# A hybrid decoder layer on one core: sample states as the fixed operand, and other orders in the MLP passages and the closing tiles

## The chip, the core and the metric

One core of a Trainium2 chip (trn2). The metric is the device time of one launch, in microseconds. A core has five engines with queues of their own that run strictly in order and wait for one another by semaphores: TensorE (PE in the profile; its weight loads are PEld), VectorE (DVE), ScalarE (ACT), GpSimd (POOL) and SyncE (SP), which only issues DMAs here.

## What is computed

A prompt of 1024 positions behind 16 learned meta positions, and 8 sample sequences that decode one position each, go through one layer: 1048 columns in all. All is float32.

```python
hn = rmsnorm(h, norm_mix);  z = hn @ w_in                 # D = 1024
u_in, c_gate, b_gate, q, k, v, g = split(z)
y_conv = b_gate * causal_conv3(c_gate * u_in)              # 512 channels
o, S = retention(rotary(q), rotary(k), v)                  # 4 heads of 128
   # prompt: chunks of 128; sample: S_b = gamma*S_b + k_b^T v_b; o_b = q_b S_b
y_ret = o * rsqrt(mean(o*o) + eps) * silu(g)               # norm per head
h = h + concat(y_conv, y_ret) @ w_out
h = h + square(relu(rmsnorm(h, norm_mlp) @ w_up)) @ w_down # D_FF = 4096
y = rmsnorm(h, norm_final)                                 # outputs, with states
```

## The kernel before

TensorE multiplies float32 in three products of a reduced format: each operand is split into a high part (ScalarE: a rounding copy) and a low part (VectorE or GpSimd: value minus high part), and hi*hi, lo*hi and hi*lo are added in PSUM.

**Heads.** A loop over four heads; each head has six units of projection times three column tiles, steps j = 0 to 17. In between stand the chunks of the retention. For the samples: ScalarE scales the eight states (j = 5), spreads the eight query columns over a table `q_smp` of 8 by 8 columns, zero off the diagonal (j = 6), and VectorE updates the states. At j = 12 TensorE runs eight float32 products with `q_smp[:, b, :]` (8 columns) as the fixed operand and a state (128 columns) as the moving one (L1748); they add up to an 8 x 128 tile, a sample a row. ScalarE copies it (L916), takes the sum of squares of each row (L917) and the roots (L922), VectorE scales it with the other rows (L1254, L1257), and TensorE turns it at j = 14 (L1760) together with nine prompt tiles (L1757). VectorE multiplies the turned tiles with the gate (L1265), for which ScalarE makes silu at j = 12, 13, 14 (L929).

**MLP.** Both projections are done as Strassen-like block products: seven products instead of eight per 2 x 2 block, here called steps i = 0 to 6. The up projection has 16 units q (`UNITS`); the down projection 8 blocks b of hidden channels (`BLOCKS`), each with four passages n (output channels), the list `DN`. So a down step has the number 7q + i, with q the passage. An up step is 24 products of 258 columns, a down step 12. A step writes into PSUM pair `BANK[i]`, (0, 1, 0, 1, 2, 1, 2), so step 2 waits until the result of step 0 has been read, step 3 for step 1, 5 for 3, 6 for 4, the next passage's 1 for 5.

The last block is cut by columns: passage n = 0 whole, then n = 1, 2, 3 for columns 0 to 258 of each half (`ts = (0,)`), then for 258 to 516.

Around each step the other engines work in an order that is written out by hand:
- ScalarE splits weights (`up_split`, `down_split`) and the middle values (`mid_split`), squares (`squared`), and reads step 0 of an up unit (L1079). `SPLITS` and `LOWS` say at which up step the weights of units 1 and 2 are split; later units follow one unit ahead. `mid_step` says at which down step the seven middle operands of the next block get their high part; the two halves of the low part (`mid_low`, VectorE, L1440) come one and two steps later. Down weights lie in two slots; those of passages 5 to 9 are split at the steps of `AHEAD`, 5.6 steps a passage, later ones two passages ahead.
- VectorE reads every step out of PSUM. In block 0 it copies step 0 into `a1` (L1581) and adds `h_in` to steps 1, 2, 3, 5 (L1585); in all other cases it adds to what is there (L1591). It also makes `mid_sum` (block sums of the middle values), `scaled` (relu and norm) and the low parts.
- GpSimd makes the block sums of the weights (L709 to L717 up, L743 to L748 down), the low parts of the down weights (L755), at the end `close` (L769: three of four results still need `a1`), and `gather` (L775).
- SyncE loads weights and middle values (`load_down`, `load_mid`) and stores.

**Closing tiles.** The result lies channel by channel; nine tiles `FINAL` of up to 128 positions are turned by eight transpositions each (L1870), squared and summed by ScalarE (L1128), rooted (L1133), and scaled by VectorE with the gain into `y_out` (L1557). Four tiles (columns 0 to 256 of both halves) run between the last products (`FINAL_AT`, `NORM_AT`), five after them, one of which gathers columns 496 to 516 of both halves.

```python
 87 FINAL_AT = {(NW, 3): 0, (NW + 1, 0): 1, (NW + 1, 5): 2, (NW + 2, 3): 3}
 88 NORM_AT = {(NW + 1, 1): 0, (NW + 1, 3): 1, (NW + 2, 1): 2, (NW + 2, 6): 3}
109     return {0: {4: 0}, 1: {1: 1, 4: 2}, 2: {1: 3, 4: 4}, 3: {1: 5, 4: 6}}[n]
136   AHEAD.setdefault(min(28 + (28 * (_wi - 5) + 4 * _i) // 5 + 1, 55), []).append((_wi, _i))
```

## Time and profile before

| | |
|---|---|
| three runs | 1168.94, 1171.07, 1172.07 us; median 1171.07 |
| profiled execution | 1170.56 us, its span 1168.8 us |
| TensorE busy | 1145.3 us, 98% of the span, 8689 products |
| weight loads (PEld) | 1119.8 us, 96% |
| VectorE, ScalarE, GpSimd busy | 764.9, 434.7, 551.0 us |
| mean granted clock | 0.996 |

The span is from the first to the last instruction. TensorE's products overlap: a product's record is 0.28 us long and the next starts 0.12 us after it, so "busy" only says that some record covers the time. A row of the timeline has start, length, engine, line, operation and tiles; in brackets, how long the engine was idle before it and who released it. Roughly: 0 to 60 us the input, to 390 the heads, to 482 the output projection, to 813 the up half, to 1154 the down half, then the closing tiles.

### The profile page before, as it was taken

The numbers are of one execution on the slowest core, as the hardware profiler recorded it, in microseconds if no ns is written. First come the engines' busy times: TensorE is split into PE (matmuls) and PEld (weight loads), VectorE is DVE, ScalarE is ACT, GpSimd is POOL, SyncE is SP. The second block draws the span as 40 slices with busy tenths as digits, with TensorE's granted clock in tenths as the row PEclk, the third lists the DMA queues.
The fourth block names the chain that finished last, engine by engine and source line by source line (L and its number), as shares of the span: only waits on it lengthen the run. The fifth ranks groups of instructions, "written<-read, shape, count | busy, mean of one in ns | idle before, by whom it ended". The sixth has DMA issues, their size and how long they took to land.

```text
span 1168.8 us, 22531 instructions
## 1 busy us (share of the span) xinstructions
PE 1145.3 (98%) x8689; PEld 1119.8 (96%) x8689; DVE 764.9 (65%) x1141; ACT 434.7 (37%) x853; POOL 551.0 (47%) x541
## 2 busy tenths in 40 slices
PE   9999999999999999989999999999999999999996
PEld 7899999999999999989999999999898999999996
DVE  4355446456355676787777776777866677777756
ACT  6423313214124433533333333335434444444413
POOL 0154242253150431044232322323989998888992
PEclk9999999999999999999999999999999999999999
DMA  6431211211201222254435353437854553454213
GB/s 202 132 110 36 79 50 54 74 54 54 74 19 57 80 89 87 74 163 134 166 118 181 109 166 130 138 120 257 277 186 129 177 169 103 146 176 136 89 38 146
DMA packets 154007, 139.79 MB, mean 120 GB/s; under 512 B 6809, under 2 KB 118146, under 8 KB 153916
## 3 DMA queue, kind: packets, MB, share of 16 engines
q1 hardware_dynamic: 148814, 135.50, 36.3%
q10 hardware_dynamic: 5102, 3.05, 0.9%
q8 instruction: 61, 1.00, 0.4%
q14 instruction: 30, 0.25, 0.1%
HBM read 98.07 MB, written 40.47 MB: 119 GB/s over the span
## 4 chain that ended last, share of the span: by engine, by line
PE 46%; POOL 3%; DVE 3%; DMA 1%; issue 1%; ACT 0%; SPq 0%; ACTq 0%; POOLq 0%; DVEq 0%
PE pair L1819 15%; PE pair L1820 15%; PE pair L1821 15%; POOL dn_lo L755 2%; DMA m_raw<-m_dram 1%; DVE m_lo L1440 1%; DVE y_out L1557 1%; PE pair L1870 0%; DVE hid L1585 0%; POOL dn_s L743 0%; DVE hid L1459 0%; POOL dn_s L745 0%; ACT m_hi L1058 0%; POOL dn_s L748 0%; POOL dn_s L746 0%
## 5 line engine op out<-in xcount | busy, mean ns | idle before, releaser
L1819 PE MATMUL pair<-m_hi,dn_hi 128*128 128x258 f32 x896 | 256.5, 286 | 8.3 <-DVE a L1591 2.8
L1819 PE MATMUL pair<-b_hi,up_hi 128*128 128x258 f32 x896 | 255.0, 285 | 3.2 <-DVE hid L1497 2.2
L1820 PE MATMUL pair<-m_lo,dn_hi 128*128 128x258 f32 x896 | 254.3, 284 | 0.0
L1821 PE MATMUL pair<-m_hi,dn_lo 128*128 128x258 f32 x896 | 254.1, 284 | 0.0
L1820 PE MATMUL pair<-b_lo,up_hi 128*128 128x258 f32 x896 | 253.6, 283 | 0.0
L1821 PE MATMUL pair<-b_hi,up_lo 128*128 128x258 f32 x896 | 252.2, 282 | 0.0
L1620 PE MATMUL pair<-x_hi,w_both 128*128 128x344 f32 (+2 forms) x576 | 188.7, 328 | 0.0
L1622 PE MATMUL pair<-x_hi,w_both 128*128 128x344 f32 (+2 forms) x576 | 184.3, 320 | 0.0
L1621 PE MATMUL pair<-x_lo,w_both 128*128 128x344 f32 (+2 forms) x576 | 184.2, 320 | 0.0
L1819 PEld LDWEIGHTS pair<-m_hi,dn_hi 128*128 128x128 f32 x896 | 169.7, 189 | 11.1 <-POOL dn_lo L755 7.9
L1591 DVE TENSOR_TENSOR hid<-pair,hid 128x516 f32<-128x516 f32 (+1 forms) x194 | 124.5, 643 | 78.9 <-PE pair L1821 77.6
L1819 PEld LDWEIGHTS pair<-b_hi,up_hi 128*128 128x128 f32 x896 | 169.1, 189 | 5.6 <-DVE up_lo L1407 3.5
L1820 PEld LDWEIGHTS pair<-m_lo,dn_hi 128*128 128x128 f32 x896 | 170.4, 190 | 0.0
L1821 PEld LDWEIGHTS pair<-m_hi,dn_lo 128*128 128x128 f32 x896 | 170.2, 190 | 0.0
L1820 PEld LDWEIGHTS pair<-b_lo,up_hi 128*128 128x128 f32 x896 | 168.9, 188 | 0.1
L1821 PEld LDWEIGHTS pair<-b_hi,up_lo 128*128 128x128 f32 x896 | 168.9, 189 | 0.0
L709 POOL TENSOR_TENSOR up_s<-up_raw 128x512 f32<-128x512 f32 x16 | 24.9, 1554 | 212.0 <-DVE up_lo L1407 139.4
L755 POOL TENSOR_TENSOR dn_lo<-dn_s,dn_hi 128x256 fp32r<-128x256 f32 x128 | 109.8, 866 | 19.4 <-ACT dn_hi L1052 19.3
L1620 PEld LDWEIGHTS pair<-x_hi,w_both 128*128 128x128 f32 x576 | 108.2, 188 | 1.6 <-issue 0.9
L1621 PEld LDWEIGHTS pair<-x_lo,w_both 128*128 128x128 f32 x576 | 108.3, 188 | 0.0
L1622 PEld LDWEIGHTS pair<-x_hi,w_both 128*128 128x128 f32 x576 | 108.2, 188 | 0.0
L1440 DVE TENSOR_TENSOR m_lo<-m_raw,m_hi 128x516 fp32r<-128x516 f32 x112 | 100.8, 904 | 8.7 <-ACT m_hi L1058 8.7
(205 smaller groups left out, 2141.4 us busy)
## 6 DMA issues: line engine op xcount, KB each, us to landing
m_raw<-m_dram SPq DMA_DIRECT2D x56, 516.0 KB, 5.0
m_dram<-hid SPq DMA_DIRECT2D x64, 258.0 KB, 2.3
up_raw<-w_up_dram SPq DMA_DIRECT2D x32, 512.0 KB, 5.0
dn_raw<-w_down_dram SPq DMA_DIRECT2D x128, 128.0 KB, 2.4
w_raw<-w_in_dram SPq DMA_DIRECT2D x28, 512.0 KB, 3.7
m_dram<-hid SPq DMA_DIRECT2D x16, 774.0 KB, 3.8
h_dram<-hid SPq DMA_DIRECT2D x8, 516.0 KB, 3.2
h_in<-h_dram SPq DMA_DIRECT2D x16, 258.0 KB, 4.3
```

The lines of the kernel that those rows point to most:

```text
L709: g.tensor_tensor(sums[0][:, :], a21, a22, ALU.add).then_inc(up_sums, 1)
L755: g.tensor_tensor(dn_lo[n][i][:, :, :], src, dn_hi[n][i][:, :, :], ALU.subtract).then_inc(dn_ready, 1)
L1440: d.tensor_tensor(m_lo[b % 2][j][:, half, :], m_raw[b % 2][j][:, half, :], m_hi[b % 2][j][:, half, :], ALU.subtract).then_inc(mid_ready, 1)
L1557: d.scalar_tensor_tensor(out=y_out[i % 4][0:rows, :].rearrange("p (h c) -> p h c", h=2), in0=final_bank(i)[0:rows, :, :], scalar=rstd_f[0: ...
L1591: d.tensor_tensor(to, src, to, ALU.add).then_inc(dn_read, 1)
L1620: m_.matmul(out, sh, mh, start=i == 0, stop=False)
L1621: m_.matmul(out, sh, ml, start=False, stop=False)
L1622: ins = m_.matmul(out, sl, mh, start=False, stop=i == len(pairs) - 1)
L1819: m_.matmul(to, shs[k], mhs[k], start=STARTS[i] and k == 0, stop=False, skip_group_check=more)
L1820: m_.matmul(to, shs[k], mls[k], start=False, stop=False, skip_group_check=more)
L1821: ins = m_.matmul(to, sls[k], mhs[k], start=False, stop=k == last, skip_group_check=more)
```

## The change

- Samples: the state is the fixed operand and one query column the moving one; eight products write a 128 x 8 tile, a sample a column. ScalarE copies and squares it, a product with a matrix of ones sums over the channels into every row (j = 13), ScalarE takes the root (j = 13, between two gates), VectorE inverts, scales and gates (j = 15). `q_smp`, the sums by row and the small transposition go.
- Up half: `SPLITS` and `LOWS` of units 1 and 2 are laid later; the first unit's middle sums come after the bank reads; in unit 1 `scaled` comes ahead of the low parts; some squares one step later.
- Down half: `MID_HIGH` and `MID_LOW` replace `mid_step`, with own lists for block 0; the copy into `a1` goes from VectorE to ScalarE; in the last up unit the splits of the middle values go by (0), (1), (2), (3), (4, 5), (6); `AHEAD` covers passages 5 to 31.
- Closing: the column cut is at 260 instead of 258; the gathered tile is columns 256 to 260 of both halves (8 positions) and comes fifth, between the products; four tiles come after them. Of the first of these six transpositions and their squares come before the last passage has ended. The norms between the products are cut in two halves.

```diff
-FINAL_AT = {(NW, 3): 0, (NW + 1, 0): 1, (NW + 1, 5): 2, (NW + 2, 3): 3}
-NORM_AT = {(NW + 1, 1): 0, (NW + 1, 3): 1, (NW + 2, 1): 2, (NW + 2, 6): 3}
+FINAL_AT = {(NW, 3): 0, (NW, 6): 1, (NW + 1, 3): 2, (NW + 1, 6): 3, (NW + 2, 2): 4}
+NORM_AT = {(NW, 6): (0, 0), (NW + 1, 0): (0, 1), (NW + 1, 2): (1, 0), (NW + 1, 3): (1, 1), (NW + 1, 6): (2, 0), (NW + 2, 0): (2, 1),
+           (NW + 2, 2): (3, 0), (NW + 2, 3): (3, 1), (NW + 2, 5): (4, 0), (NW + 2, 6): (4, 1)}
+EARLY_AT = (NW + 2, 4)
...
+MID_HIGH = ({11: 0, 13: 1, 15: 2, 17: 3, 20: 4, 22: 5, 24: 6}, {4: 0, 6: 1, 8: 2, 12: 3, 15: 4, 19: 5, 22: 6})
+MID_LOW = ({12: 0, 15: 1, 17: 2, 19: 3, 22: 4, 24: 5, 26: 6}, {6: 0, 9: 1, 12: 2, 16: 3, 19: 4, 23: 5, 26: 6})
...
+for _wi in range(5, NW):
     for _i in range(7):
+        AHEAD.setdefault(max(30 + 62 * (_wi - 5) // 10 + 55 * _i // 100, 7 * (_wi - 2) + _i), []).append((_wi, _i))
...
+EDGE = (0, 2 * P + 4, HALF)
+FINAL = [(l, c, c + P) for l in range(2) for c in (0, P)] + [(None, 2 * P, EDGE[1]), (0, EDGE[1], 388), (1, EDGE[1], 388), (1, 388, HALF), (0, 388, HALF)]
+REST, FIRST_LATE = 4, 5
+EARLY_F, LATE_F = (0, 1, 2, 4, 5, 6), (3, 7)
...
 # ScalarE, heads
+                            act.wait_ge(smp_done, 2 * h + 1)
+                            s.activation(o_smp[:, :], SMP_B[:, 0:SAMPLES], ACT.Copy)
+                            s.activation(sq_smp[:, :], SMP_B[:, 0:SAMPLES], ACT.Square).then_inc(smp_read, 1)
...
+                        if j == 13:
+                            act.wait_ge(smp_done, 2 * h + 2)
+                            s.activation(std_smp[:, :], SMP_B[:, SAMPLES:2 * SAMPLES], ACT.Sqrt, scale=1.0 / DK, bias=eps).then_inc(smp_read, 1)
...
 # ScalarE, up half and down half
-                      (0, 6): (), (1, 0): ((1, 4), (1, 5)), (1, 1): ((1, 6), (2, 0)), (1, 2): ((2, 1),), (1, 3): ((2, 2),), (1, 4): ((2, 3), (2, 4))}
+                      (0, 6): ((1, 4), (1, 5), (1, 6)), (1, 0): (), (1, 1): ((2, 0),), (1, 2): (), (1, 3): (), (1, 4): ((2, 1), (2, 2)), (1, 5): ((2, 3), (2, 4)),
+                      (1, 6): ((2, 5), (2, 6))}
...
-                        if i:
-                            mid_split(i - 1)
+                        for j in ((), (0,), (1,), (2,), (3,), (4, 5), (6,))[i]:
+                            mid_split(j)
...
+                    if b == 0 and i == 0:
+                        act.wait_ge(dn_done, 7 * q + 1)
+                        s.activation(a1[:, n, :].rearrange("p (t c) -> p t c", c=TQ), pair[BANK[0]][:, :, 0:TQ], ACT.Copy).then_inc(a1_copied, 1)
...
 # VectorE, up half
-                    (1, 0): ((1, 4), (1, 5)), (1, 1): ((1, 6), (2, 0)), (1, 2): ((2, 1),), (1, 3): ((2, 2),), (1, 4): ((2, 3), (2, 4))}
+                    (1, 0): (), (1, 1): ((1, 4), (1, 5)), (1, 2): ((1, 6), (2, 0)), (1, 3): (), (1, 4): ((2, 1), (2, 2)), (1, 5): ((2, 3), (2, 4)),
+                    (1, 6): ((2, 5), (2, 6))}
...
-                    if q == 1 and i < 3:
-                        for j in ((0, 1), (2,), (3,))[i]:
-                            mid_sum(0, j)
...
+                    if q == 1 and i in (1, 2):
+                        mid_sum(0, 2 * i - 2)
+                        mid_sum(0, 2 * i - 1)
...
 # VectorE, down half
-                        d.tensor_copy(to, src).then_inc(dn_read, 1)
+                        dve.wait_ge(a1_copied, q + 1)
...
-                    if q == 0 and i < 2:
-                        mid_low(5 + i, 0)
-                        mid_low(5 + i, 1)
-                    if q == 0 and i == 2:
+                    if q == 0 and i < 4:
+                        mid_low(5 + i // 2, i % 2)
+                    if q == 0 and i == 4:
                         scaled(LASTU, 3)
...
 # TensorE
-                                ins = m_.matmul(SMP_B[0:SAMPLES, 0:P], q_smp[:, b, :], state[:, b, :], start=b == 0, stop=b == SAMPLES - 1)
+                                ins = m_.matmul(SMP_B[:, b:b + 1], state[:, b, :], q_rot[:, PROMPT + b:PROMPT + b + 1], start=True, stop=True)
...
+                        if j == 13:
+                            pe.wait_ge(smp_read, 2 * h + 1)
+                            m_.matmul(SMP_B[:, SAMPLES:2 * SAMPLES], ones[:, :], sq_smp[:, :], start=True, stop=True).then_inc(smp_done, 1)
...
-                            m_.transpose(S_B[:, TAIL:TAIL + SAMPLES], o_smp[0:SAMPLES, :], ident[0:SAMPLES, 0:SAMPLES]).then_inc(yT_done, 1)
...
+                if early:
+                    pe.wait_ge(closed, 18)
+                    pe.wait_ge(dn_read, 7 * (ND - 1))
```

## Rows read from the trace of the kernel before

**Rows 1.** Stretches: us, busy time (instructions) of each engine, granted clock, DMA share, GB/s.

```profile
560.00:790.00 230.00, 230.00 (x1899) 228.39 (x1898) 170.66 (x226) 79.92 (x135) 69.06 (x44) 1.00 0.40 136
905.00:915.00 10.00, 7.45 (x49) 7.48 (x50) 5.09 (x8) 3.75 (x10) 9.78 (x14) 0.83 0.69 217
```

**Rows 2.** TensorE's waits in 10:530, 800:860, 860:1000: us in total, times, longest.

```profile
PE pair L1819 <- DVE hid L1497: 2.2, 1, 2.2
...
PE pair L1819 <- DVE hid L1490: 1.0, 1, 1.0
...
PE pair L1819 <- DVE hid L1585: 2.7, 4, 0.9
PE pair L1819 <- DVE hid L1591: 0.7, 1, 0.7
PE pair L1819 <- DVE a L1581: 0.5, 1, 0.5
...
PE pair L1819 <- DVE a L1591: 2.8, 1, 2.8
PE pair L1819 <- DVE hid L1591: 1.2, 2, 0.9
```

**Rows 3.** Timeline of TensorE, around two waits.

```profile
817.03 0.36 PE L1819 MATMUL pair<-m_hi,dn_hi 128*128 128x258 f32 x1 [0.51 <-DVE a L1581]
...
898.18 0.28 PE L1821 MATMUL pair<-m_hi,dn_lo 128*128 128x258 f32 x1
898.78 0.36 PE L1819 MATMUL pair<-m_hi,dn_hi 128*128 128x258 f32 x1 [0.33 <-DVE hid L1591]
```

**Rows 4.** Timeline of ScalarE in the second up unit.

```profile
520.25 0.63 ACT L1013 ACTIVATE up_hi<-up_s 128x512 fp32r<-128x512 f32 x1 [2.88 <-POOL up_s L712]
```

**Rows 5.** Timelines of ScalarE and VectorE ahead of the wait at 907 us.

```profile
903.04 0.42 ACT L1052 ACTIVATE dn_hi<-dn_s 128x256 fp32r<-128x256 f32 x1 [5.66 <-POOL dn_s L745]
...
904.45 1.14 DVE L1440 TENSOR_TENSOR m_lo<-m_raw,m_hi 128x516 fp32r<-128x516 f32 x1 [3.26 <-ACT m_hi L1058]
```

**Rows 6.** Groups of ScalarE by line: count, busy us, mean ns, idle before.

```profile
L1079 ACT ACTIVATE hid<-pair 128x516 f32<-128x516 f32 x16 | 9.4, 585 | 0.7 <-PE pair L1821 0.7
...
L929 ACT ACT_TABLE_LOAD x4 | 5.1, 1283 | 0.1
```

**Rows 7.** Timeline of ScalarE, end of the up half and second down block.

```profile
814.49 0.64 ACT L1064 ACTIVATE hid<-hid 128x516 f32<-128x516 f32 x1 [0.52 <-DVE hid L1459]
...
816.60 1.05 ACT L1058 ACTIVATE m_hi<-m_raw 128x1032 fp32r<-128x1032 f32 x1
...
868.32 1.07 ACT L1058 ACTIVATE m_hi<-m_raw 128x1032 fp32r<-128x1032 f32 x1 [4.45 <-DMA m_raw<-m_dram]
```

**Rows 8.** Timeline of GpSimd: first sums of two passages that follow each other.

```profile
882.18 1.01 POOL L743 TENSOR_TENSOR dn_s<-dn_raw 128x256 f32<-128x256 f32 x1
...
891.88 1.29 POOL L743 TENSOR_TENSOR dn_s<-dn_raw 128x256 f32<-128x256 f32 x1
```

**Rows 9.** First head, samples: timelines of TensorE and ScalarE; groups of loads by form.

```profile
124.04 1.91 PE L1748 MATMUL pair<-state,q_smp 128*8 128x128 f32 x16
125.88 0.42 PE L1620 MATMUL pair<-x_hi,w_both 128*128 128x344 f32 x1
...
134.57 0.49 ACT L929 ACTIVATE y_raw<-y_raw  x1 [2.92 <-DVE y_raw L1288]
...
L1710 PEld LDWEIGHTS pair<-v,s_msk 128*128 128x128 f32 x64 | 11.1, 188 | 0.0
...
L1748 PEld LDWEIGHTS pair<-state,q_smp 128*8 128x8 f32 x64 | 5.4, 90 | 1.9 <-issue 0.8
```

**Rows 10.** Closing tiles: timelines of TensorE and VectorE.

```profile
1155.39 1.06 PE L1870 MATMUL pair<-ident,hid 128*128 128x128 f32 x8 [0.57 <-issue]
...
1158.17 1.28 DVE L1557 SCALAR_TENSOR_TENSOR y_out<-pair,small,gain_f 128x1024 f32<-128x1024 f32 x1
...
1163.71 1.28 DVE L1557 SCALAR_TENSOR_TENSOR y_out<-pair,small,gain_f 112x1024 f32<-112x1024 f32 x1
```

More of the change, by code:

```diff
@@ L1518, in _ @@
                         up_low(0, 5)
-                    if q == 1 and i < 3:
-                        for j in ((0, 1), (2,), (3,))[i]:
-                            mid_sum(0, j)
+                    if q == 1 and i >= 4:
+                        scaled(q, i - 3)
                     if q < LASTU:
@@ L1867, in final_transposes @@
                     pe.wait_ge(gathered, 16)
-                for f in range(KT):
+                for f in fs:
                     src = rest_f[:, f, :] if l is None else acc(f % 4, 2 * (f // 4) + l)[:, c0:c1]
@@ L1899, in _ @@
                         final_transposes(FINAL_AT[(q, i)])
-            for i in range(4, len(FINAL)):
+                    if (q, i) == EARLY_AT:
+                        final_transposes(FIRST_LATE, EARLY_F, True)
+            final_transposes(FIRST_LATE, LATE_F)
+            for i in range(FIRST_LATE + 1, len(FINAL)):
                 final_transposes(i)
```

204 lines of the change are left out of this document (110 added, 94 removed).

## The prediction

> **What bounds the kernel now.** I read the stretches first, then the list of TensorE's waits stretch by stretch, then the timelines of the queues behind the longest ones. The profiled span is 1168.8 us and the profiled execution took 1170.56, 0.5 under the median of 1171.07; all sums are differences, made on the trace and applied to the median. In the stretches TensorE is busy end to end: 1899 products in 230.00 us, 0.121 us apart [rows 1]. A step of the MLP (one of its seven block products) is 24 such products in the up half (2.9 us) and 12 in the down half (1.45 us), and nothing but fewer products or fewer gaps makes it shorter. So the kernel is TensorE's work plus its gaps plus what follows its last product.
>
> The gaps are few [rows 2]: in the up half 2.2 + 1.0 us, both in the second unit; between 800 and 860 us (the first block of the down projection) 2.7 + 0.7 + 0.5 in six waits; between 860 and 1000 us 2.8 + 1.2 in three. Each costs more than its idle time: the product at 898.78 is listed with 0.33 us of idleness, but its predecessor started 0.60 before it where 0.12 is usual, and its record is 0.36 long instead of 0.28, the pipe filling again [rows 3]. So a wait costs its idle time plus 0.15 and 0.08, say 0.24 us. The longest also costs clock: in the 10 us around it the granted clock is 0.83, so about 3.4 us at the lower level (1.2 instead of 2.4 GHz) after an idle stretch of 2.8 us, 1.7 us lost [rows 1].
>
> Who is late? In every wait VectorE's read of a PSUM bank is named, but it had the data. At 520.25 ScalarE had stood 2.88 us at a high part of the up weights, because GpSimd's block sum of unit 2 came late [rows 4]; VectorE's low part waited for that high part, and the read that TensorE wanted stood behind. At 904.45 the same: ScalarE stood 5.66 us at a down-weight split that wanted GpSimd's sum, the split of the next block's middle values stood behind it, VectorE's low part waited 3.26 us for that, and the bank reads stood behind the low part [rows 5]. These are orders in three in-order queues, not lack of an engine.
>
> **The change, part by part.**
> *Up orders.* Units 1 and 2 are split later, and the first middle sums come after the bank read. The low parts that needed unit 2's sums move from step (1, 1) to (1, 4) and later. GpSimd gets its sums started at the same point (it waits for the four middle sums, which still end in step 2), some 3 us before they are now asked for. Both waits go: 3.2 + 2 x 0.24 = **-3.7 us**. Next in line is VectorE's own length in step 2, which has room because a step is 2.9 us.
>
> *First block of the down half.* VectorE's copy of each passage's first product goes to ScalarE (0.585 us for a tile of this kind [rows 6]), the low parts leave passages 0 and 1, and each high part comes one step before its low part. Now lost: 3.9 + 6 x 0.24 = 5.3 us. What the copy brings in its place: it joins ScalarE's queue behind the splits of middle values. In the trace the last of these starts at 816.60, in a queue that was held 0.52 us at 814.49 [rows 7]; two splits now come earlier and fill that hole, and one weight split (0.3) goes behind the copy. The copy then ends near 816.60 + 0.95 - 0.52 - 0.3 + 0.585 = 817.3. TensorE wants the bank at 816.36 (it started at 817.03 [rows 3] after 0.51 idle and 0.16 of drain). So one wait stays, as 817.4 - 816.36 + 0.08 = 1.1 us. In passages 1 to 3 the item ahead of the copy is a weight split that waits for the product just before, so the copy is in time (0.585 in a step of 1.45). **-4.2 us**.
>
> *Second block and after.* High parts move up by two to three steps against their low parts, and the weight splits of passages 5 to 31 are spread at 6.2 steps each instead of 5.6, so ScalarE stands less at GpSimd's sums and VectorE finds the high parts made. Lost now: 4.0 + 3 x 0.24 + 1.7 of clock = 6.4 us. What is late next is GpSimd itself: it needs 9.7 us from one passage's first sum to the next [rows 8], against seven steps, 10.1 us, of TensorE. Until now TensorE's own gaps gave it room, 5.3 us in the first block alone. I follow it from passage 4: its weights for passage 6 would come within half a microsecond of the moment they are wanted. I book 0.6 us of waiting (ends 0 and 3.0: none, or one idle of GpSimd like the 4.45 us for which ScalarE stood at a middle load at 868.32 [rows 7], less what TensorE would spare). **-5.8 us**.
>
> *Sample states.* Now 16 records (8 products, two passes) from 124.04 to the next product at 125.88, 1.84 us, 0.115 each [rows 9]. They stream 128 columns past 8 fixed ones; afterwards they stream one column past 128. The records of the loads give the price: 188 ns with 128 columns, 90 with 8, so 0.82 ns a column [rows 9], 105 ns for 128 if all but the column part overlaps. So 16 x 0.11 = 1.8 us: the streaming is gone and the load has taken its place. Ends: a load not overlapped at all, 16 x 0.188 = 3.0 us, +1.2 a head; a load hidden completely, leaving a fill of 0.3 us, -1.5 a head. I take the middle, since the loads of the kernel's other products, same size, run 0.121 apart and overlapped [rows 1]. The product with ones adds two records and one more change of form (125.88 shows 0.26 before the next product where 0.16 is usual), 0.4 us, and one small transposition, 0.13, goes. +0.3 a head, four heads, nothing else to hide in: **+1.2 us** (ends -6.0 and +6.0). ScalarE gets two more table loads a head, 1.28 us each [rows 6], because the sample root now comes between two gates. It stands 2.92 us before the head's third gate [rows 9], which covers the 2.6, so I cost them at nothing; if that cover were gone the gates would be late by up to 2.6 us a head and VectorE's gate products with them.
> The Trainium skill ("TensorE: Matmul & The Clock Gate", section "LDWEIGHTS (loading the stationary operand)") says that a load takes its columns divided by 1.2 ns and does not depend on the rows. The rows here agree (0.82 ns a column). By that page alone this block would be 16 x 107 ns = 1.7 us, and the product's one column would buy nothing; it speaks against this part.
>
> *Closing tiles.* After the last bank read the closing work was: eight transpositions at 1155.39, first scaled tile at 1158.17, fifth at 1163.71, 1.385 apart [rows 10]. Now four tiles stay behind instead of five (-1.4), and of the first only two transpositions and a quarter of the squares are left (-0.7 and -0.6, less 0.1 for the extra step). In exchange a fifth tile (1.0 us) and six transpositions (0.8) stand between the products, and those six wait for a PSUM pair until VectorE has scaled tile 3 two halves later, some 0.4 us. Net **-0.4 us** (ends -1.5 and +1.5).
>
> Sum: -3.7 - 4.2 - 5.8 + 1.2 - 0.4 = -12.9 us: **1158.2 us**.
>
> **Rivals.**
> A. GpSimd bounds the blocks 1 and 2, since its room is spent: TensorE waits for weights, 3 us more, and if one such wait is long the low clock comes back with 1.7. For: 9.7 against 10.1 us, and it also has idle spells. Against: it gains 0.4 us a passage. 1158.2 + 4.7 = 1162.9.
> B. Loads hide completely behind each other and the sample block nearly vanishes: 1158.2 - 7 = 1151. Against: 98 ns of the load's record grow with its columns [rows 9], and no row shows two such loads at once.
> C. The sample block is not overlapped: 1158.2 + 4.8 = 1163.0.
> D. The orders only move the waits: the queues are as full as before, and three quarters of the gaps stand elsewhere. Only a quarter of 15.4, less the heads' loss: 1171.07 - 3.9 + 1.2 - 0.4 = 1168. Against: in both long stalls the blocked item was not needed for several steps.
> E. Slower. ScalarE's copy is caught behind a split that waits for a middle load. Such a wait has been 4.45 us [rows 7]. TensorE can spare one step, so each such passage costs 4.45 + 0.585 + 0.24 - 1.45 = 3.8 us and 1.7 of clock; four passages 22 us, in place of the 1.1 booked: 1179. It turns the sign if the copies are late by about 3.4 us each. Against: no high part stands right before a copy in the new lists (11, 13, 15, 17, 20, 22, 24 against copies at 0, 7, 14, 21).
>
> **How the numbers follow.** Forecast 0.60, A 0.13, B 0.06, C 0.05, D 0.10, E 0.06. A change of under 0.3% (3.5 us) can't be told from none here: faster is under 1167.6. Faster are the forecast, A, B, C: 0.84, and half of D's spread: 0.88. Same: 0.07. Slower: 0.05. The range: the forecast's own terms spread it by 3 us each way, A and C lie at 1163, half of B's at 1153. From 1152.5 to 1164.5, which leaves out D, E and the rest of B.
>
> **What would show it.** TensorE's waits near 514 and 522 us gone; in the first block one wait, for ScalarE's copy, under 1 us of idleness; none above 1 us after 860 us, and a granted clock of 1.00 there. The sample records 0.10 to 0.12 us apart and a head 0.3 us longer. Four scaled tiles after the last product, the first about 1.5 us after the last transpositions began. The forecast is wrong if a wait of TensorE for weights or for the copy exceeds 2 us, if the clock falls anywhere after the start and before the closing tiles, or if the sample block takes over 2.3 or under 1.2 us.

## The result, and the profile after

The changed kernel takes 1164.85 us (median of 4 runs, 1162.94 to 1166.66). The kernel before, beside it, took 1171.57. The ratio is 0.9945, 95% interval 0.992 to 0.9969: 6.4 us faster, between 3.6 and 9.4. The forecast was 1158.2, range 1152.5 to 1164.5. The direction was right and the result is just outside the range; half of the expected gain is missing.

| | before | after |
|---|---|---|
| profiled execution, its span | 1170.56, 1168.8 us | 1166.66, 1164.9 us |
| first product of the up half | 482.41 | 482.40 |
| up half, to the first product of the down half | 331.04 | 332.11 |
| passages 0 to 3 (336 products) | 45.80 | 43.03 |
| passages 4 to 27 | 249.33 | 247.00 |
| from passage 28 to the last product | 45.96 | 47.57 |
| last product to the end of the span | 14.26 | 12.79 |
| mean granted clock | 0.996 | 0.995 |

The stretches are differences between the starts of products in the two timelines, rounded to 0.01 us. They sum to -3.9 us, which is what the spans show. The profiled execution is the slowest of the changed kernel's four, so the median gained more than the trace explains. Two things vary from one execution to the next: the start (the up half began at 481.3 to 482.9 in the profiles of this study) and whether the clock falls at one wait of the down half (below).

TensorE's waits in the changed kernel, as the list of waits gives them (total, times, longest); they answer to those of [rows 2]:

```profile
PE pair L1865 <- DVE hid L1511: 3.0, 1, 3.0
PE pair L1706 <- DVE wv_lo L1202: 1.9, 1, 1.9
PE pair L1865 <- DVE a L1635: 1.8, 1, 1.8
PE pair L1865 <- DVE hid L1629: 1.3, 1, 1.3
PE pair L1865 <- ACT a L1125: 0.7, 1, 0.7
```

Lines 1865 to 1867 are now the products, 1511 the read of step 1 in the up half, 1629 and 1635 reads in the down half, 1125 ScalarE's new copy. None of the MLP's waits of before stands where it stood; one in the first block is now for ScalarE's copy, as forecast, and three longer ones stand elsewhere (the 1.9 us at wv_lo are in the start, where it was 1.2 before). The stretches around the two longest:

```profile
533.00:543.00 10.00, 6.98 (x46) 6.80 (x45) 6.76 (x10) 1.79 (x3) 0.54 (x1) 0.83 0.72 237
950.00:960.00 10.00, 8.24 (x56) 8.06 (x56) 5.67 (x8) 5.93 (x13) 9.78 (x13) 0.83 0.61 189
```

(Columns: start and end of the stretch, length, busy time and records of PE, PEld, DVE, ACT, POOL, then granted clock, DMA share, GB/s.) In both the granted clock is 0.83, as it was around 907 us before [rows 1]: each wait costs another 1.4 us, since 15 products follow 0.21 us apart instead of 0.12.

**The wait at 537 us.** VectorE and GpSimd, changed kernel, timelines of the stretch before it:

```profile
526.31 0.69 DVE L1534 TENSOR_TENSOR hid<-pair,hid 128x516 f32<-128x516 f32 x1
527.03 1.35 DVE L1479 SCALAR_TENSOR_TENSOR hid<-hid,r_all 128x516 f32<-128x516 f32 x1
528.30 1.78 DVE L1427 TENSOR_TENSOR up_lo<-up_raw,up_hi 128x512 fp32r<-128x512 f32 x1
530.01 1.77 DVE L1427 TENSOR_TENSOR up_lo<-up_s,up_hi 128x512 fp32r<-128x512 f32 x1
531.70 0.68 DVE L1489 TENSOR_TENSOR hid<-hid 128x516 f32<-128x516 f32 x1
532.42 1.68 DVE L1492 TENSOR_TENSOR hid<-hid 128x516 f32<-128x516 f32 x1
534.01 0.68 DVE L1494 TENSOR_TENSOR hid<-hid 128x516 f32<-128x516 f32 x1
534.62 0.68 DVE L1497 TENSOR_TENSOR hid<-hid 128x516 f32<-128x516 f32 x1
535.23 0.68 DVE L1427 TENSOR_TENSOR up_lo<-up_raw,up_hi 128x512 fp32r<-128x512 f32 x1
535.83 0.68 DVE L1511 TENSOR_TENSOR hid<-pair,hid 128x516 f32<-128x516 f32 x1
```
```profile
526.53 1.29 POOL L724 TENSOR_TENSOR up_s<-up_raw 128x512 f32<-128x512 f32 x1 [3.83 <-DVE up_lo L1427]
527.97 1.57 POOL L727 TENSOR_TENSOR up_s<-up_s,up_raw 128x512 f32<-128x512 f32 x1
529.49 1.73 POOL L729 TENSOR_TENSOR up_s<-up_raw 128x512 f32<-128x512 f32 x1
531.86 1.69 POOL L732 TENSOR_TENSOR up_s<-up_raw,up_s 128x512 f32<-128x512 f32 x1 [0.63 <-DVE up_lo L1427]
```

VectorE has no idle time here. Eight operations stand between the last read of unit 1 and the read that TensorE wants (535.83), and four of them take 1.35 to 1.78 us instead of 0.68. The four slow ones lie beside GpSimd's sums for unit 3, and each ends 0.54 to 0.56 us after the sum beside it. In the kernel before this queue was shorter by one operation: the low part of (2, 5) stood one step earlier, while that of (2, 6), the scaled tile and the four middle sums stood here already. There too the read was only just in time:

```profile
536.35 0.68 DVE L1490 TENSOR_TENSOR hid<-pair,hid 128x516 f32<-128x516 f32 x1
537.18 0.36 PE L1819 MATMUL pair<-b_hi,up_hi 128*128 128x258 f32 x1
```

These two are of the kernel before. The product starts 0.15 us after the read's end, as it does behind the wait (536.51 to 536.66), and 0.14 us after its predecessor where 0.12 is usual. So the read had no room, and any time that TensorE gained ahead of it had to be gained by this read as well.

**The wait at 954 us.** ScalarE, VectorE and TensorE, changed kernel:

```profile
941.93 0.42 ACT L1059 ACTIVATE dn_hi<-dn_s 128x256 fp32r<-128x256 f32 x1 [5.74 <-POOL dn_s L760]
949.92 0.42 ACT L1059 ACTIVATE dn_hi<-dn_s 128x256 fp32r<-128x256 f32 x1 [5.63 <-POOL dn_s L760]
950.95 1.05 ACT L1065 ACTIVATE m_hi<-m_raw 128x1032 fp32r<-128x1032 f32 x1
952.03 1.15 DVE L1460 TENSOR_TENSOR m_lo<-m_raw,m_hi 128x516 fp32r<-128x516 f32 x1 [2.04 <-ACT m_hi L1065]
953.10 0.68 DVE L1635 TENSOR_TENSOR a<-pair,a 128x516 f32<-128x516 f32 x1
953.93 0.35 PE L1865 MATMUL pair<-m_hi,dn_hi 128*128 128x258 f32 x1 [1.76 <-DVE a L1635]
```

This is the chain of [rows 5] again, 47 us later: a weight split that wants GpSimd's sum, a split of middle values behind it, a low part that waits for that, a read behind the low part.

**The wait at 821 us.** VectorE's read was ready to go and its second operand, the transfer of h_in, was not there; SyncE had issued it at 817.05, and it landed at 820.32. In the kernel before it had landed at 818.63, 0.2 us ahead of the read. The changed kernel:

```profile
817.05 1.76 SPq L572 DMA_DIRECT2D h_in<-h_dram  x4
820.42 0.70 DVE L1629 TENSOR_TENSOR hid<-pair,h_in 128x516 f32<-128x516 f32 x1 [1.42 <-DMA h_in<-h_dram]
```

**The sample block and the product with ones** (TensorE, head 0; they answer to [rows 9]), and **the closing**:

```profile
124.10 0.32 PE L1666 MATMUL pair<-x_hi,w_both 128*128 128x344 f32 x1
124.25 1.84 PE L1792 MATMUL pair<-q_rot,state 128*128 128x1 f32 x16
125.95 0.41 PE L1664 MATMUL pair<-x_hi,w_both 128*128 128x344 f32 x1
129.82 0.28 PE L1796 MATMUL pair<-sq_smp,ones 128*128 128x8 f32 x2
129.96 0.40 PE L1664 MATMUL pair<-x_hi,w_both 128*128 128x344 f32 x1
130.21 0.32 PE L1665 MATMUL pair<-x_lo,w_both 128*128 128x344 f32 x1
```
```profile
1152.23 0.74 DVE L1587 SCALAR_TENSOR_TENSOR y_out<-pair,small,gain_f 8x512 f32<-8x512 f32 x1
1152.89 0.40 DVE L1635 TENSOR_TENSOR hid<-pair,hid 128x256 f32<-128x256 f32 x1
1153.40 3.03 PE L1921 MATMUL pair<-ident,hid 128*128 128x128 f32 x26 [1.01 <-issue]
1154.87 1.28 DVE L1582 SCALAR_TENSOR_TENSOR y_out<-pair,small,gain_f 128x1024 f32<-128x1024 f32 x1
1159.17 1.28 DVE L1582 SCALAR_TENSOR_TENSOR y_out<-pair,small,gain_f 128x1024 f32<-128x1024 f32 x1
```

The first fence shows the block at 1.70 us to the next product. The second shows the first and the last of four closing tiles, the first 1.47 us after the transpositions began, and the last bank read (1152.89) behind half a scaled tile.

### The profile page after: what moved, and what is told of

Same layout as the page of the kernel before. It is cut to its first block, busy times and chain, and to the rows that moved or that the text cites. A ratio compares the mean times of both kernels' runs of the same rounds, so it can differ in the third digit from the quotient of the medians.

```text
span 1164.9 us, 22579 instructions
## 1 busy us (share of the span) xinstructions
PE 1144.3 (98%) x8693; PEld 1122.9 (96%) x8693; DVE 765.6 (66%) x1147; ACT 442.5 (38%) x859; POOL 554.7 (48%) x540
## 4 chain that ended last, share of the span: by engine, by line
PE 82%; POOL 10%; DVE 3%; DMA 1%; issue 1%; ACT 1%; SPq 0%; POOLq 0%; ACTq 0%; DVEq 0%
PE pair L1865 14%; PE pair L1866 14%; PE pair L1867 14%; PE pair L1664 8%; PE pair L1666 8%; PE pair L1665 8%; POOL dn_lo L770 7%; PE pair L1842 3%; PE pair L1844 3%; PE pair L1843 3%; PE pair L1706 1%; PE pair L1707 1%; PE pair L1709 1%; POOL dn_s L760 1%; POOL dn_s L758 1%
## 5 line engine op out<-in xcount | busy, mean ns | idle before, releaser
L1865 PE MATMUL pair<-m_hi,dn_hi 128*128 128x258 f32 (+2 forms) x896 | 256.3, 286 | 3.8 <-DVE a L1635 1.8
L1866 PE MATMUL pair<-m_lo,dn_hi 128*128 128x258 f32 (+2 forms) x896 | 254.3, 284 | 0.0
L1867 PE MATMUL pair<-m_hi,dn_lo 128*128 128x258 f32 (+2 forms) x896 | 254.0, 283 | 0.0
L1635 DVE TENSOR_TENSOR hid<-pair,hid 128x516 f32<-128x516 f32 (+2 forms) x194 | 124.6, 643 | 79.2 <-PE pair L1867 77.4
```

The source lines that it names most:

```text
L1635: d.tensor_tensor(to, src, to, ALU.add).then_inc(dn_read, 1)
L1865: m_.matmul(to, shs[k], mhs[k], start=STARTS[i] and k == 0, stop=False, skip_group_check=more)
L1866: m_.matmul(to, shs[k], mls[k], start=False, stop=False, skip_group_check=more)
L1867: ins = m_.matmul(to, sls[k], mhs[k], start=False, stop=k == last, skip_group_check=more)
```

## Experiments

All are edits of the changed kernel. A ratio is to the kernel before, run beside it; the changed kernel's is 0.9945. "Up" and "down" are the two halves' lengths as in the table (332.11 and 337.60 in the changed kernel's profile). A median of four runs carries about 2 us of uncertainty, so single effects are read from the timelines.

**1. The up half's orders put back.**

```diff
-                      (0, 6): ((1, 4), (1, 5), (1, 6)), (1, 0): (), (1, 1): ((2, 0),), (1, 2): (), (1, 3): (), (1, 4): ((2, 1), (2, 2)), (1, 5): ((2, 3), (2, 4)),
-                      (1, 6): ((2, 5), (2, 6))}
+                      (0, 6): (), (1, 0): ((1, 4), (1, 5)), (1, 1): ((1, 6), (2, 0)), (1, 2): ((2, 1),), (1, 3): ((2, 2),), (1, 4): ((2, 3), (2, 4))}
...
```

The lists of the low parts and the places of `squared`, `mid_sum` and `scaled` go back in the same way.

> The changed kernel with the orders of the up half (splits, low parts, squares, middle sums, scaled tiles of units 0 to 2) put back as they were; all else of the change stays. Theory 1 (the new orders removed the waits at 514 and 522 us, 3.7 us, and brought a longer one of 3.2 us and 1.4 us of low clock at 537 us): the 537 us wait is gone, waits of about 2.2 and 1.0 us are back near 514 and 522 us, and the down half starts about 1.0 us earlier than in the changed kernel (813.5); the time is 1.0 us under the changed kernel's, so 7.5 to 8 us under the kernel before. Theory 2 (the wait at 537 us comes from elsewhere, from GpSimd being late by itself or from a state of this one execution): it is still there beside the two old ones, and the down half starts 3.7 us later than in the changed kernel, near 818.

1163.81 us, ratio 0.9952 (0.9935 to 0.9968). Up 331.12: 1.0 us shorter. The wait at 537 is gone and the old ones stand at 513.33 (0.97) and 521.58 (2.22). This is theory 1. The new orders of the up half cost 1.0 us where the forecast had them gain 3.7; the times of the runs, which don't tell the two kernels apart, can't show so little.

**2. Reads first in unit 2.**

```diff
-                    if i == 0 and q > 1:
+                    if i == 0 and q > 2:
                         for j in range(4):
                             mid_sum(q - 1, j)
...
-                    if q == 1 and i in (1, 2):
-                        mid_sum(0, 2 * i - 2)
-                        mid_sum(0, 2 * i - 1)
+                    if q in (1, 2) and i in (1, 2):
+                        mid_sum(q - 1, 2 * i - 2)
+                        mid_sum(q - 1, 2 * i - 1)
```

> The changed kernel with one move: in unit 2 the four middle sums of unit 1 no longer stand ahead of step 1's bank read on VectorE, but two behind that read and two behind step 2's. Theory 1 (the wait of 3.0 us at 537 us is VectorE's backlog: six operations of 0.7 to 1.8 us stand ahead of the read that TensorE waits for): moving four of them, 2.9 us in the trace, behind the read takes the wait to under 0.5 us and the clock's dip with it, so the down half starts 3.5 to 4.6 us earlier (810 to 811) and the time is 3.5 to 4.6 us lower. Theory 2 (VectorE is short of time over the whole of unit 2, beside GpSimd's sums that slow its operations): the wait only moves one or two steps on, to the read of step 3 or 4, with at least 2 us; the down half starts under 1.5 us earlier.

1159.74 us, ratio 0.991 (0.9894 to 0.9927). Up 327.96, 4.15 us shorter. In the same ten microseconds as above the granted clock is 1.00, and what is left is one wait:

```profile
533.00:543.00 10.00, 9.51 (x80) 9.33 (x79) 7.86 (x14) 3.58 (x6) 1.89 (x2) 1.00 0.69 232
```
```profile
539.16 0.36 PE L1865 MATMUL pair<-b_hi,up_hi 128*128 128x258 f32 x1 [0.49 <-DVE hid L1518]
```

This is theory 1: the wait was a matter of a place in a queue. Against the old orders (331.12) it is -3.2 us, so most of the forecast's -3.7 was there to be had.

**3. Weight splits at an even distance.**

```diff
-        AHEAD.setdefault(max(30 + 62 * (_wi - 5) // 10 + 55 * _i // 100, 7 * (_wi - 2) + _i), []).append((_wi, _i))
+        AHEAD.setdefault(max(28 + _i // 2, 7 * _wi + _i - 10), []).append((_wi, _i))
```

> The changed kernel with the weight splits of passages 6 to 31 issued ten steps ahead of their use throughout, instead of five steps growing to fourteen. Theory 1 (from passage 15 on ScalarE asks for GpSimd's sum some 5.6 us before it can be there, stands at it in each passage, and the splits of the next block's middle values stand behind; the wait at 954 us is that): ScalarE's stand per passage falls below 1 us, the wait of 1.8 us at 954 us and its dip in the clock go, and the time is about 3.3 us under the changed kernel's. Theory 2 (GpSimd is simply the slower engine, 8.5 to 9.8 us a passage against TensorE's 10.1): asking later makes it later still; TensorE waits for dn_lo tiles after 860 us, by more than 1 us in all, and the time is equal or higher.

1162.83 us, ratio 0.9939 (0.9919 to 0.9958). The forecast of 3.3 us does not show in the ratio (0.7 us); the timeline shows more. Passages 4 to 27 take 242.97 us, which is what 2016 products 0.1205 apart take (242.9): no gap is left there, 4.0 us less than in the changed kernel's profile, 1.3 to 2.0 less than in the profiles of runs 1, 2, 4, 6 and 10, which keep its orders there. Theory 1 is right about the wait and wrong about why. ScalarE did not stop standing; up to 976 us it stood for GpSimd 2.3 to 6.2 us at a stretch in every passage, as here:

```profile
938.48 0.42 ACT L1059 ACTIVATE dn_hi<-dn_s 128x256 fp32r<-128x256 f32 x1 [6.17 <-POOL dn_s L760]
```

Up to there GpSimd sets the splits' pace (most of its passages take 8.5 to 9.9 us), however early or late ScalarE asks; from about 1030 us on it has caught up and follows TensorE's 10.1. The moment of the stand against the lists of middle values is what counts. Theory 2 fell: TensorE did not wait for dn_lo after 860 us.

**4. The residual's loads earlier.**

```diff
+            for n in range(KT):
+                sp.wait_ge(h_saved[n], 16)
+            for i in range(4):
+                load_h(0, i)
             store_row(LASTU, 6)
             store_row(LASTU, 2)
-            for n in range(KT):
-                sp.wait_ge(h_saved[n], 16)
-            for i in range(4):
-                load_h(0, i)
```

> The changed kernel with the four loads of h_in for passage 0 issued ahead of the last two row stores on SyncE's queue, instead of behind them. Theory 1 (the 1.3 us wait at 821 us is that transfer: it is issued at 817.0, lands at 820.4, and VectorE sat idle 1.4 us for it): the loads are issued 3 us or more earlier, VectorE's read of step 1 starts at 818.5 to 819, TensorE's wait at 821 falls under 0.3 us, and the time is 1.0 to 1.5 us lower. Theory 2 (behind the transfer the low parts of the middle values are as late, as in the kernel before): a wait of 0.7 us or more stays there, named for VectorE, and the time falls by under 0.7 us.

1163.57 us, ratio 0.9942 (0.9926 to 0.9959). The wait at 821 is gone, but one of 0.98 us is new at 854.40, so passages 0 to 3 take 42.55 instead of 43.03. Theory 1 has the place but not the price: the time does not fall by 1.0 to 1.5 us, since most of it was lost again 33 us later. How much remains is uncertain, as seven profiles with the changed kernel's loads and lists in the first block spread from 42.77 to 43.96 us. Ahead of the new wait VectorE had stood 1.09 us for a high part of the middle values, and ScalarE for the transfer of that part:

```profile
851.23 1.07 ACT L1065 ACTIVATE m_hi<-m_raw 128x1032 fp32r<-128x1032 f32 x1 [4.07 <-DMA m_raw<-m_dram]
```

**5. Five moves together**: runs 2, 3 and 4, and two more. The last split of middle values and the last weight split of passage 0 leave step 6 of the last up unit and stand behind ScalarE's first copy; `load_mid` goes ahead of `load_h`.

```diff
+                        if q == 0:
+                            mid_split(6)
+                            down_split(0, 6)
...
+                if b < BLOCKS - 1:
+                    for j in ((2,), (3, 4), (5, 6), ())[n] if b == 0 else ((0, 1, 2), (3, 4), (5, 6), ())[n]:
+                        load_mid(7 * (b + 1) + j)
                 if b == 0 and n < 3:
                     for i in range(4):
                         load_h(n + 1, i)
```

> The changed kernel with five moves together: the reads of unit 2 first, the loads of h_in earlier, the splits of passages 6 to 31 ten steps ahead, and two new ones: in the first down passage ScalarE copies the first product before the last split of middle values and the last weight split of passage 0, and SyncE issues the loads of the next block's middle values ahead of those of h_in. Theory 1 (each remaining wait is a place in a queue and they add): against the changed kernel -4.1 (unit 2), -1.4 (h_in), -0.9 (copy), -1.5 to -3.3 (wait at 954 us), and the new wait near 855 us, 0.8 to 1.1 in the runs with one move, does not come: 8 to 9.5 us in all, a ratio to the kernel before of 0.986 to 0.9875, with no wait of TensorE over 0.5 us between 482 us and the closing tiles. Theory 2 (GpSimd sets the pace of the down half: 9.7 us a passage, and ScalarE still stood 2.3 to 6.2 us at its sums when it asked later): with TensorE's own gaps gone it waits for dn_lo tiles, 1 us or more in all, and the sum of the moves falls short by as much.

1158.20 us, ratio 0.9897 (0.988 to 0.9913): 5.6 us under the changed kernel by the ratios, 8.1 by the spans of the profiled executions. Up 328.10, down 333.31. The copy's wait is gone, and from 860 to 1100 us TensorE is busy throughout:

```profile
860.00:1100.00 240.00, 240.00 (x1994) 239.98 (x1992) 180.52 (x250) 104.30 (x215) 230.00 (x274) 1.00 0.48 148
```

Theory 2 fell, though GpSimd is busy 230 of 240 us. The waits that theory 1 named went, but its sum was not reached: the ratio was to be 0.986 to 0.9875, and no wait was to exceed 0.5 us. A wait of 1.4 us came in the first block: the loads of h_in, now behind those of the middle values, landed 5.1 to 7.7 us after their issue between 820 and 850 us, where the median over the changed kernel was 3.9:

```profile
846.50 0.70 DVE L1633 TENSOR_TENSOR hid<-pair,h_in 128x516 f32<-128x516 f32 x1 [3.26 <-DMA h_in<-h_dram]
```

**6. The copy back on VectorE.**

```diff
-                        s.activation(a1[:, n, :].rearrange("p (t c) -> p t c", c=TQ), pair[BANK[0]][:, :, 0:TQ], ACT.Copy).then_inc(a1_copied, 1)
...
+                        d.tensor_copy(to, src).then_inc(dn_read, 1)
```

> The changed kernel with the copy of each passage's first product in block 0 back on VectorE. Theory 1 (the copy on ScalarE is a part that pays: VectorE has too much in the first block, and the copy adds 0.6 us a passage ahead of the reads TensorE wants): the wait near 818 for ScalarE's copy (0.7 to 1.3 us) goes, but VectorE's waits in passages 0 to 3 come back, 2 us or more in at least three waits; net 1 to 2 us slower than the changed kernel. Theory 2 (what helped the first block is only that the low parts left passages 0 and 1): the 818 wait goes and nothing over 0.5 us takes its place; 0.5 to 1.3 us faster than the changed kernel.

1164.54 us, ratio 0.9952 (0.9934 to 0.9969), which can't be told from the changed kernel's. Passages 0 to 3 take 44.02 us against 42.77 to 43.96 with ScalarE's copy. This is neither theory: three waits (1.03, 0.54, 1.18 us) take the place of two or three. The move of the copy is worth at most 1.3 us.

**7. The old distances, 8. the old lists of the middle values**, each alone.

```diff
-        AHEAD.setdefault(max(30 + 62 * (_wi - 5) // 10 + 55 * _i // 100, 7 * (_wi - 2) + _i), []).append((_wi, _i))
+        AHEAD.setdefault(min(28 + (28 * (_wi - 5) + 4 * _i) // 5 + 1, 55) if _wi < 10 else 7 * (_wi - 2) + _i, []).append((_wi, _i))
```
```diff
-MID_HIGH = ({11: 0, 13: 1, 15: 2, 17: 3, 20: 4, 22: 5, 24: 6}, {4: 0, 6: 1, 8: 2, 12: 3, 15: 4, 19: 5, 22: 6})
-MID_LOW = ({12: 0, 15: 1, 17: 2, 19: 3, 22: 4, 24: 5, 26: 6}, {6: 0, 9: 1, 12: 2, 16: 3, 19: 4, 23: 5, 26: 6})
+MID_HIGH = ({4: 0, 8: 1, 11: 2, 15: 3, 18: 4, 22: 5, 25: 6},) * 2
+MID_LOW = ({5: 0, 9: 1, 12: 2, 16: 3, 19: 4, 23: 5, 26: 6},) * 2
```

> The changed kernel with the old distances of the weight splits (passages 5 to 9 at 5.6 steps each, from passage 10 on two passages ahead), and the new lists of the middle values. Theory 1 (the stall of the kernel before at 904 us stood where its ramp ended, passage 9, as the changed kernel's at 954 us stands where its ramp ends, passage 15; the ramp places it): the wait at 954 goes and one of 1 to 3 us comes back between 895 and 910 us; time within 1 us of the changed kernel's. Theory 2 (the lists of the middle values, with two to three steps between a high part and its low part, removed the stall at 904): no wait over 0.5 us between 860 and 920 us; the one at 954 stays or goes with the ramp.

> The changed kernel with the old lists of the middle values in the down half (each high part one step before its low part, in passages 0 to 3 alike), and the new distances of the weight splits. Theory 1 (the high part behind GpSimd's sum stalls whatever the low part's distance, since ScalarE stands 5.6 us there): waits as long as or longer than the 1.8 us of 954 us appear, at two or more places after 860 us, each with a dip of the clock when over 1.5 us, and low parts are back in passage 0, with 1.5 to 2.5 us of waits: 3 to 6 us slower than the changed kernel. Theory 2 (the distances of the weight splits alone did it): no wait over 1 us after 860 us beyond that at 954; under 2 us slower.

Old distances: 1168.51 us, ratio 0.998 (0.9969 to 0.9991). Passages 4 to 27 take 248.66 us. The wait at 954 is gone and two long ones stand earlier again, the second with a dip of the clock and 6 us behind the stretch that theory 1 named:

```profile
897.82 0.36 PE L1865 MATMUL pair<-m_hi,dn_hi 128*128 128x258 f32 x1 [1.49 <-DVE hid L1635]
916.19 0.36 PE L1865 MATMUL pair<-m_hi,dn_hi 128*128 128x258 f32 x1 [2.25 <-DVE a L1635]
```

Old lists: 1167.63 us, ratio 0.997 (0.9955 to 0.9985). Passages 0 to 3 take 45.94 us, waits of 0.4 to 1.2 us among them, and one of 1.76 us without a dip stands at 936.41; passages 4 to 27 take 245.75.

For the distances theory 1 has the mechanism: their ramp (the stretch of passages over which the splits run further and further ahead) decides where the stall stands. For the lists it is half right: the low parts hold the first block, but after 860 us one wait came and not two or more, and most of the loss is in the first block. The sizes: without the new distances the kernel is 4 us slower, not within 1; without the new lists it is 3 us slower by the ratios, and there the two intervals overlap, so that only the first block's 45.94 against 42.77 to 43.96 us shows it.

**9. Six moves, 12. five moves mended.**

```diff
+                    if q == 2 and i == 2:
+                        mid_sum(1, 2)
+                        mid_sum(1, 3)
...
+                    if b == 0 and n < 3:
+                        load_h(n + 1, 0)
+                        load_h(n + 1, 1)
```

The first part, ahead of step 2's low part, is in both; the second, ahead of `load_down`, in run 9 alone.

> The kernel with five moves, with two of them refined: in unit 2 the last two middle sums stand ahead of step 2's low part, which waits for ScalarE, and SyncE issues the first two loads of h_in for the next passage ahead of the down weights, then the middle values, then the last two of h_in. Theory 1 (the 1.4 us wait at 847 us was the transfer of h_in, issued behind six others and landing 7 us later, and the 0.5 us at 540 us the order of one low part): both fall under 0.3 us, the time is 1.5 to 2 us under that with five moves, so a ratio to the kernel before of 0.9875 to 0.989. Theory 2 (the queues of the 16 DMA engines are full in the first block, so that one transfer or another is late whatever the order): a wait of 0.7 to 1.5 us appears between 830 and 860 us at another transfer, and the time falls by under 0.8 us.

> The kernel with five moves, and of the sixth run's two refinements only that in unit 2 (the last two middle sums ahead of step 2's low part); the loads of h_in go back to one group behind the middle values. Theory 1 (the two halves add: 327.3 us for the up half as with six moves, 333.3 us for the down half as with five): 0.8 us under the kernel with five moves, a ratio to the kernel before of 0.989, and one wait of 1.2 to 1.6 us near 847 us as there. Theory 2 (the time the up half gains is lost in the first block, where transfers are the limit): the down half takes 334 us or more, and the time is that with five moves within 0.3 us.

Run 9: 1158.53 us, ratio 0.9887 (0.9871 to 0.9904). Run 12: 1158.99 us, ratio 0.989 (0.9872 to 0.9907). The up half gains 0.8 us in both (327.32, 327.33), and the down half gives it back: 334.64 and 334.51 against 333.31 in run 5. In run 9 the waits are 0.80 us at 849.20, where VectorE sat idle 1.51 us for h_in, and 1.10 us at 866.79, behind a high part for whose m_raw ScalarE had waited 3.94 us. That is theory 2: a transfer in or just behind the first block is late, and its place moves with the order of issue. In run 12 the down half is as long as theory 2 said, but only 0.5 of its 1.2 us are lost in passages 0 to 3 (43.17 against 42.63, with a wait of 1.51 us at 847.53). The rest is a wait of 0.62 us at 988.66, and no transfer stands behind it: a low part of VectorE took 2.10 us instead of 0.68 while GpSimd made low parts of its own.

```profile
985.80 2.10 DVE L1464 TENSOR_TENSOR m_lo<-m_raw,m_hi 128x516 fp32r<-128x516 f32 x1
```

The three kernels can't be told apart in time. They are 12 to 13 us under the kernel before and 5.5 to 7 under the changed one.

**10. Sample products with 64 columns.**

```diff
-  m_.matmul(SMP_B[:, b:b + 1], state[:, b, :], q_rot[:, PROMPT + b:PROMPT + b + 1], start=True, stop=True)
+  m_.matmul(SMP_B[:, 0:64], state[:, b, :], q_rot[:, PROMPT - 56:PROMPT + 8], start=True, stop=True)
```

> The changed kernel with each sample product streaming 64 query columns past the state instead of one (64 of the tile's other columns, so the samples' part of the output is another). Theory 1 (a record of this block takes the time of its load of 128 columns, about 0.106 us, and what streams past is hidden up to some 64 columns): the block of 16 records still takes 1.70 us to the next product, within 0.1. Theory 2 (the pitch is streaming and a fixed part per product, as in the kernel before, where 128 columns past a load of 8 took 0.115 a record): each record grows by half the streaming, 0.02 to 0.05 us, and the block takes 2.0 to 2.5 us.

One execution, 1163.56 us; the samples' outputs come out different, as the edit means. The block starts at 124.10 and the next product at 125.81:

```profile
124.10 1.89 PE L1792 MATMUL pair<-q_rot,state 128*128 128x64 f32 x16
125.81 0.41 PE L1664 MATMUL pair<-x_hi,w_both 128*128 128x344 f32 x1
```

1.71 us with 64 columns, 1.70 with one. Theory 2 fell: moving columns up to 64 cost nothing here. The time is what theory 1 said, 0.106 us a record on average, but that the load sets it is not shown. A load of 8 columns with 128 moving ones gave 0.115 a record before, so a floor of about 0.11 us a record, whatever is loaded, would fit as well.

**11. GpSimd's sums for unit 3 later.**

```diff
+                if u == 3 and i == 0:
+                    pool.wait_ge(up_read, 11)
```

> The changed kernel with one wait more: GpSimd begins the block sums of unit 3 (526.5 to 533.5 us) only behind VectorE's read of step 1 in unit 2. Theory 1 (VectorE's operations there take 1.3 to 1.8 us instead of 0.68 because GpSimd's sums run beside them): the scaled tile and the two low parts of 527 to 532 us take 0.7 us each, the read of step 1 starts some 2.5 to 3 us earlier and the wait at 537 us as such goes; the splits of unit 3 are late instead, so a wait of 1 us or more may come at a later step. Theory 2 (those operations are slow for another reason, their operands or their PSUM tiles): they keep 1.3 to 1.8 us each and the wait at 537 us stays at 3 us.

One execution, 1162.02 us, up 329.08. The same three operations of VectorE, with GpSimd silent until 532.34:

```profile
526.26 0.69 DVE L1481 SCALAR_TENSOR_TENSOR hid<-hid,r_all 128x516 f32<-128x516 f32 x1
526.88 0.68 DVE L1429 TENSOR_TENSOR up_lo<-up_raw,up_hi 128x512 fp32r<-128x512 f32 x1
527.48 0.68 DVE L1429 TENSOR_TENSOR up_lo<-up_s,up_hi 128x512 fp32r<-128x512 f32 x1
```

0.69, 0.68, 0.68 us instead of 1.35, 1.78, 1.77. This is theory 1. The read of step 1 starts at 531.52 instead of 535.83 (3.5 us earlier, counted from the first product of the up half), and the new wait is 1.47 us at 540.13, since the sums are late for step 3.

## Why the prediction was wrong

Forecast -12.9 us; measured -3.9 between the profiled executions and -6.4 by the ratio. Of its own signs of being wrong one came: the clock fell, after the waits at 537 and 954 us. By its steps, from the timelines:

**Up orders, -3.7: the step that failed.** The two waits went, as foreseen, and -3.7 became +1.0. The sentence at fault is "next in line is VectorE's own length in step 2, which has room because a step is 2.9 us". It gave that queue no price and looked at unit 1, where the change was made. There was no room: in the kernel before, the read of step 1 in unit 2 ended at 537.03 and TensorE's product followed at once. With TensorE 3.7 us earlier this read had to come 3.7 us earlier too, and it came 0.5 us earlier (535.83 against 536.35). Two things held it: the four middle sums that stand ahead of it, and GpSimd's sums, beside which an operation of VectorE with two SBUF operands takes up to 1.78 us. The work moved down from unit 1's early steps made this queue one low part longer. Run 2 moves the middle sums and wins 4.15 us, run 11 moves GpSimd's sums and wins 3.0. Both were in the trace of the kernel before: a scaled tile beside GpSimd's sum took 1.78 us there.

```profile
527.87 1.78 DVE L1459 SCALAR_TENSOR_TENSOR hid<-hid,r_all 128x516 f32<-128x516 f32 x1
```
```profile
527.33 1.76 POOL L712 TENSOR_TENSOR up_s<-up_s,up_raw 128x512 f32<-128x512 f32 x1
```

The Trainium skill ("SBUF — State Buffer", section "Who interferes with whom") says that a VectorE instruction with two inputs in SBUF contends with a GpSimd instruction that reads SBUF, and it calls the port pair that the two engines share an exclusive lock. The trace agrees: the read of a PSUM bank at 526.31 kept its 0.69 us, the four with both inputs in SBUF did not, and each of these ended 0.54 to 0.56 us after GpSimd's operation beside it. By this rule, the forecast would have had to add what was left of GpSimd's operation to each of VectorE's that starts beside it.

**First block, -4.2: measured -2.8.** The copy's wait came near its size, 0.70 us idle and 0.86 lost against 1.1 (1.0 by the forecast's own terms, which put the copy's end at 817.3 and not 817.4), with some luck: in seven other profiles with the same order there it is 0.36 to 1.49 us idle. What was missed is the read behind it. I took VectorE's low parts for the only thing in its way; with them gone the read waited for h_in, and TensorE 1.31 us for the read. That transfer had landed 0.2 us ahead of the read in the kernel before; there it was hidden behind an engine that was later still.

**Second block and after, -5.8: measured -2.3,** and -4.3 to -5.1 in the other profiles with the same orders but for run 11 (244.3 to 245.0 us in runs 1, 2, 4, 6 and 10), where the wait at 954 is 1.0 to 1.3 us and the clock does not fall. The waits at 877, 898 and 907 went. In their place I booked 0.6 us for GpSimd as the slower engine; it is its sum, asked too early at the end of the ramp, that stalls ScalarE and with it the middle values. Runs 3 and 7 show that the ramp places it: passages 5 to 9 before, 5 to 15 now. Run 3 also shows that the forecast gain was there to be had: without the ramp these passages take 6.4 us less than before.

**Sample states, +1.2: measured -0.3.** Sixteen records took 1.70 us against 1.8. Run 10 confirms that the streaming was gone from the price; that the load took its place stays argued. A head is 80.87 us against 80.95. The product with ones cost 0.22 us (129.67 to 130.21 less two usual pitches), not 0.4, and I had not noticed that the old block began 0.24 us after its predecessor instead of 0.16. The two extra table loads a head cost nothing that shows in a head's time, as booked. This miss went the other way by 1.5 us and so hid a part of the others in the total. The Trainium skill ("TensorE: Matmul & The Clock Gate", section "LDWEIGHTS (loading the stationary operand)") has a load take its columns divided by 1.2 ns, which gives an estimate of 1.7 us for this block. The trace agrees with 1.70.

**Closing tiles, -0.4: measured +0.1.** Between the products +1.6 (2.2 booked), behind the last -1.5 (2.6 booked). The first tile is as early as foreseen after its transpositions. But these began 1.29 us after the last product instead of 0.85, behind a last bank read that stood behind half a scaled tile of 0.74 us, and the end of the span lies 0.6 us further behind the last tile than before. The last store was issued as the tile ended in both, and the span ended 4.4 us later instead of 3.8; why was not followed up.

Of the rivals, D (the orders only move the waits, 1168, 0.10) had the mechanism, in two places of three. It deserved more than 0.10: its counter-argument, that the blocked item was not needed for several steps, held for the items looked at and said nothing of what they would stand in front of next. A was half right: GpSimd's sums made the new stall, but through ScalarE and the middle values, not by TensorE waiting for weights. E did not come.

## What to carry to other kernels

When work is moved down an in-order queue, write out that queue where it arrives, with each operation at its price beside what the other engines do at that time, and mark the item that the bounding engine wants. A wait that is removed uncovers the next operand of the same instruction: ask of each read not only which engine holds it up but when its transfers land. Where two engines run at nearly the same pace, changing how far ahead one asks moves the stall in time; only what stands behind the stall can be taken out of its way.

## What the runs showed of the hardware

- VectorE's operations with two SBUF operands (128x512 and 128x516) took 0.68 to 0.70 us alone and 1.35 to 1.78 beside GpSimd's sums in the changed kernel; one took 2.10 beside GpSimd's low parts in run 12. GpSimd's sums (128x512) took 1.28 to 1.29 alone and up to 1.76 beside VectorE.
- With 128 fixed columns, sixteen records took 1.70 us with one moving column and 1.71 with 64: 0.106 us a record in both.
- Idle spells of TensorE of 3.0, 2.8 and 2.25 us were followed by a dip of the granted clock that cost 1.3 to 2.5 us beyond the idle time and the usual 0.24; spells of 2.2 us at 522 us, in the kernel before and in run 1, were not. One of 1.76 us was followed by a dip in the changed kernel (953.93) and by none in run 8 (936.41), so the idle spell alone does not decide it.
- Transfers of the same 258 KB, the rows of h_in, landed 2.6 to 8.2 us after issue. The four for passage 0 took 3.3 to 4.2 us when issued at 817 to 818 us in the changed kernel, and 6.9 to 7.3 when issued at 809 to 811 us in run 4, right behind the loads of the down weights. In the first block (814 to 860 us) of the changed kernel the DMA share is 0.83.
